# Spreading the second layer's decay rows with rounded-fp32 matmuls on 40 partitions

## The reference, cut to what matters

```
cum = jnp.cumsum(log_a.astype(jnp.float32).reshape(b, h, n, CHUNK), axis=-1)
decay = jnp.exp(jnp.where(lower, cum[..., :, None] - cum[..., None, :], -jnp.inf))
scores = jnp.einsum('bhnid,bhnjd->bhnij', qc, kc) * decay
y_intra = jnp.einsum('bhnij,bhnjv->bhniv', scores, vc)
```

## Time and profile before

| | us |
|---|---|
| median of 3 runs | 1595.27 |
| lowest and highest of them | 1591.41, 1597.74 |
| the profiled execution | 1586.63 |
| its span, first to last instruction | 1584.8 |
| PE busy in the span | 1465.9 |
| the second layer's mixer, from the first spread to the output projection | about 673 to 757 |
| mean granted TensorE clock, share of 2.4 GHz | 0.959 |

### The profile page before, as it was taken

How to read it: one execution, slowest core, us unless ns; L and a number is a source line. 1 busy time by engine, 2 the same in 40 slices (tenths; PEclk the granted TensorE clock), 3 DMA queues, 4 the chain that set the end, 5 groups by cost and what they waited for, 6 DMA issues and landing times.

```text
span 1584.8 us, 22300 instructions
## 1 busy us (share of the span) xinstructions
PE 1465.9 (92%) x8816; PEld 1227.8 (77%) x8816; DVE 933.9 (59%) x1539; ACT 669.0 (42%) x1079; POOL 783.5 (49%) x359
## 2 busy tenths in 40 slices
PE   5999878999989998885999999999999989899997
PEld 3878678999978887442778888888878854799997
DVE  3687657878786687557676544431127687634433
ACT  3446544454543233555342222222226366454443
POOL 0533315888844443644334444444444540478885
PEclk9999988999989999966999999999999999999999
DMA  9657405777765652000236555543333330345664
GB/s 369 232 196 268 159 11 183 245 254 246 250 221 177 196 161 89 19 27 1 80 114 217 187 186 186 186 140 98 97 98 100 105 100 1 107 148 186 186 182 124
DMA packets 71319, 242.96 MB, mean 153 GB/s; under 512 B 7472, under 2 KB 13104, under 8 KB 70832
## 3 DMA queue, kind: packets, MB, share of 16 engines
q1 hardware_dynamic: 68800, 237.15, 44.8%
q10 hardware_dynamic: 2416, 4.39, 0.9%
HBM read 239.42 MB, written 1.05 MB: 152 GB/s over the span
## 4 chain that ended last, share of the span: by engine, by line
PE 49%; DVE 5%; ACT 2%; issue 1%; POOL 1%; DMA 0%; DVEq 0%; ACTq 0%
PE bank L513 13%; PE bank L515 13%; PE bank L514 13%; PE bank L923 1%; POOL w_lo L1729 1%; PE cond_a L983 1%; DVE sq_sum L1843 1%; PE bank L646 1%; PE bank L647 1%; PE bank L650 1%; PE cond_b L1001 1%; PE cond_b L931 1%; DVE h_lo L1786 0%; PE bank L943 0%; PE cond_b L943 0%
## 5 line engine op out<-in xcount | busy, mean ns | idle before, releaser
L1729 POOL TENSOR_TENSOR w_lo<-raw,w_hi 128x1024 fp32r<-128x1024 f32 (+3 forms) x306 | 721.5, 2366 | 739.7 <-ACT w_hi L1231 724.7
L1231 ACT ACTIVATE w_hi<-raw 128x1024 fp32r<-128x1024 f32 (+3 forms) x301 | 309.4, 1030 | 598.6 <-PE bank L515 541.0
L513 PE MATMUL bank<-h_hi,w_hi 128*128 128x256 f32 (+2 forms) x1604 | 529.6, 330 | 8.8 <-POOL w_lo L1729 5.4
L514 PE MATMUL bank<-h_lo,w_hi 128*128 128x256 f32 (+2 forms) x1604 | 525.9, 328 | 0.0
L515 PE MATMUL bank<-h_hi,w_lo 128*128 128x256 f32 (+2 forms) x1604 | 525.8, 328 | 0.0
L513 PEld LDWEIGHTS bank<-h_hi,w_hi 128*128 128x128 f32 (+1 forms) x1604 | 301.9, 188 | 45.6 <-POOL w_lo L1729 6.4
L515 PEld LDWEIGHTS bank<-h_hi,w_lo 128*128 128x128 f32 (+1 forms) x1604 | 301.9, 188 | 30.2
L514 PEld LDWEIGHTS bank<-h_lo,w_hi 128*128 128x128 f32 (+1 forms) x1604 | 302.1, 188 | 29.9
L1786 DVE TENSOR_TENSOR hidden_lo<-work,hidden_hi 128x256 fp32r<-128x256 f32 (+1 forms) x66 | 113.2, 1715 | 162.2 <-ACT hidden_hi L1303 162.2
L513 PE MATMUL bank<-hidden_hi,w_hi 128*128 128x256 f32 (+1 forms) x528 | 168.7, 320 | 0.6 <-POOL w_lo L1729 0.6
L514 PE MATMUL bank<-hidden_lo,w_hi 128*128 128x256 f32 (+1 forms) x528 | 168.5, 319 | 0.0
(11 more groups left out here) (399 smaller groups left out, 1899.2 us busy)
## 6 DMA issues: line engine op xcount, KB each, us to landing
raw<-in_up SPq DMA_DIRECT2D x132, 512.0 KB, 3.6
ada_w<-in_ada SPq DMA_DIRECT2D x128, 512.0 KB, 4.5
raw<-in_down SPq DMA_DIRECT2D x48, 448.0 KB, 3.4
raw<-in_out SPq DMA_DIRECT2D x24, 512.0 KB, 3.6
raw<-in_down SPq DMA_DIRECT2D x24, 512.0 KB, 3.5
raw<-in_in SPq DMA_DIRECT2D x24, 512.0 KB, 3.6
arena<-in_ada SPq DMA_DIRECT2D x16, 512.0 KB, 11.8
raw<-in_uq SPq DMA_DIRECT2D x12, 384.0 KB, 3.0
```

Of the source, the lines that this page charges most:

```text
L513: pe.matmul(out, w_h, x_h, start=first, stop=False)
L514: pe.matmul(out, w_h, x_l, start=False, stop=False)
L1231: act.activation(part_slot(w_hi, f, u), raw_slot(f, u), ACT.Copy).then_inc(s["rounded"], 1)
L1729: pool.tensor_tensor(part_slot(w_lo, f, u), raw_slot(f, u), part_slot(w_hi, f, u).bitcast(F32), ALU.subtract).then_inc(s["split"], 1)
```

## The change

The rows of sums are split into a rounded high part and the low part that the rounding leaves, as is done for the weights, and both are spread by one fp32r matmul.

- PE makes the rows twice: for each 128 tokens one plain-fp32 matmul writes output partitions 0 to 31 (it takes 32 columns of the sums, of which the first 8 are the wanted ones), and one writes the same 8 rows to partitions 32 to 39. So 16 matmuls stand in place of 8.
- DVE copies 40 partitions instead of 8 into `grow`, which is now a view of fp32r type on the same memory (`work_r`), waits for its own second copy, and then subtracts the rounded rows from PSUM on partitions 32 to 39, in two instructions of 8x512.
- A new tensor `picks` (128x8, fp32r) is the sum of two slices of the identity: its column h is 1 on partitions h and 32 + h. The DVE instruction that makes it stands ahead of its wait for the running sums.
- `spread` takes column h of `picks[0:40]` and `grow[0:40]`: fp32r by fp32r, 40 partitions.

```diff
+        pick_rows = sbr("picks", [P, RH])
...
+        with nc.sbuf_tensor("work_r", [P, 3, TOK], F32R) as work_r:
+            pass
         work = sb("work", [P, 3, TOK])
...
-        gs, ngs = c(2, TT, RH), c(2, TT, RH)
+        sums_flat = c(4 * TT * RH)
+        gs, ngs = (sums_flat[:, 64 * a:64 * a + 64].rearrange("p (d i h) -> p d i h", d=2, i=TT) for a in range(2))
         v_mean, gn_inv, sq_2 = c(2, 4), c(32), c(512)
-        grow, dt_rows = work[:, 0:2, :], std
+        grow, dt_rows = work_r[:, 0:2, :], std
+        picks = pick_rows[:, :]
...
-                    pe.matmul(decay_bank(q)[:, :], ident[0:RH, h:h + 1].to_broadcast([RH, P]), grow[0:RH, d, :],
+                    pe.matmul(decay_bank(q)[:, :], picks[0:40, h:h + 1].to_broadcast([40, P]), grow[0:40, d, :],
                               start=True, stop=True).then_inc(s["sd_b"], 1)
...
-                        last = pe.matmul(bank[6 + d][0:RH, i * P:(i + 1) * P], gs[:, d, i, :], ident,
+                        n = (TT * d + i) * RH
+                        pe.matmul(bank[6 + d][0:32, i * P:(i + 1) * P], sums_flat[:, n:n + 32], ident,
+                                  start=True, stop=True)
+                        last = pe.matmul(bank[6 + d][32:40, i * P:(i + 1) * P], sums_flat[:, n:n + RH], ident,
                                          start=True, stop=True)
...
                 vr_products(5, 8)
+                then(dve.tensor_tensor(picks, ident[:, 0:RH], ident[:, 32:32 + RH], ALU.add))
                 dve.wait_ge(s["cum_ready"], 2)
...
-                copy(grow[0:RH, 0, :], bank[6][0:RH, :])
-                copy(grow[0:RH, 1, :], bank[7][0:RH, :]).then_inc(s["rows_taken"], 1)
+                copy(grow[0:40, 0, :], bank[6][0:40, :])
+                then(copy(grow[0:40, 1, :], bank[7][0:40, :]))
+                low(grow[32:40, 0, :], bank[6][32:40, :], grow[32:40, 0, :])
+                low(grow[32:40, 1, :], bank[7][32:40, :], grow[32:40, 1, :]).then_inc(s["rows_taken"], 1)
```

## The result

The changed kernel takes 1580.05 us (median of six runs, 1566.88 to 1584.44); the kernel before, on the same chip, takes 1594.49 (six runs, 1591.41 to 1599.77). The ratio is 0.9896, with a 95% interval from 0.9853 to 0.9939. By it the change is worth 16.6 us of 1594.49 (the two medians lie 14.4 apart), and the forecast was 6.5. Two later repetitions gave 0.992 and 0.9911, so 13 to 17 us is what has to be explained.

The account below looks back on a forecast made before the run. Hand-overs between engines, on a chain through PE's spreads, bound the mixer, with no engine full. Savings 3.30 + 0.24 + 2.03 + 1.06 = 6.6 us, costs 0, 6.5 with hand-overs: 1595.27 - 6.5 = 1588.8 us, range 1582 to 1595.

Parts of the forecast that it names:

- price of `picks`: One small DVE instruction of 0.17 us, placed where DVE idles 0.60 us waiting for PE: cost 0, at most 0.1 us.
- walk along the chain: Second layer's mixer, 672 to 757 us, in four pieces, asking what is late next: 6.6 us saved together.
- q = 4, 5: Mixer spreads, 692 to 707 us: DVE is late next, so of 1.3 us only 0.24 arrives.
- q = 8, 11: Mixer spreads, 707 to 722 us: an idle DVE waits for each, so 2.03 us arrives.
- q = 0 to 3: First mixer spreads, 672 to 692 us: PE runs without a gap, so all 3.30 us arrives.
- q = 12, 15: Mixer spreads, 722 to 757 us: 0.66 us, then about 0.4 as POOL is late next; sum 1.06.
- Price of one spread: A spread on the chain goes from 1.05 to 0.40 us at 2.4 GHz, from 2.07 to 0.71 at 1.2.
- Rows, subtractions, `picks`: Added PE and DVE work: DVE 1.45 us later, within its 1.70 us wait for POOL (the cover); cost 0, bounds to 3.4.
- higher bound of 1.75 us: Extra PE time for the rows if their 32 records run one after the other; the sum took 0.1 us instead.
- more of it at 1.2 GHz: Rival: more mixer spreads at 1.2 GHz, each saving 1.36 instead of 0.65 us; 8 to 11.5 us less, chance 0.25.
- the clock falls instead: Rival: shorter spreads leave the mixer's 2.4 GHz stretches at 1.2 GHz; net +5.5 us, 1601, chance 0.05.
- The signs: Expected after: 16 L1006 records, 0.2 us DVE wait, first spread at 673.3, stretch to L513 from 83.4 to about 77 us.

Follow-up runs that it names:

- e1: The kernel before plus one unused 32-byte tensor where the change puts `picks`, no instruction changed; ratio to the kernel before 0.996.
- e9: The changed kernel plus 64 more unused bytes behind `picks`, 96 in all; 1572.69 us against 1592.45 for the kernel before, ratio 0.9878.
- e4: The kernel before plus an unused tensor of 64 bytes in the place of `picks`; ratio to the kernel before 0.9965.
- e6: The change with `picks` behind all other tensors (old addresses), but spreads left plain fp32 on 8 partitions; ratio to the kernel before 1.0009.
- e2: The whole change with `picks` allocated behind `spare`, so all other tensors keep their old addresses; ratio to the kernel before 0.9941.
- e3: The changed kernel measured again, unaltered; ratio to the kernel before 0.992.
- e11: The changed kernel measured a third time, unaltered; 1580.78 us, ratio to the kernel before 0.9911.
- e10: The kernel before plus 32 unused bytes ahead of the weights, so weights and all else move together; ratio to the kernel before 1.0001.
- run 32: Not a run label: in "run 32 records in the 1.9 us", "run" is a verb and 32 counts matmul records.

## Why the prediction was wrong

Two terms failed. The price of `picks`, put at 0 and at most 0.1 us, took its one DVE instruction and left out its 32 bytes, which moved the operands of the dense matmuls: measured alone (e1), 6.4 us. And the walk along the chain, 6.6 us, kept all work between the spreads at its old duration, and let 0.24 and 2.03 us arrive at q = 4, 5 and q = 8, 11 where 0.9 and 2.5 did: the mixer got 9.4 us shorter.

**The walk.** In the table "long" is the mean of the eight traces with plain fp32 spreads, "short" of the five of the change. The pieces end at the prediction's borders: the first `group_spread` (692), `ssd_weighted` of pair 0 (707), `ssd_scores` of pair 1 (722), L513.

| piece | long | short | gained | forecast |
|---|---|---|---|---|
| q = 0 to 3 | 19.0 | 14.0 | 5.0 | 3.30 |
| q = 4, 5 | 15.8 | 14.9 | 0.9 | 0.24 |
| q = 8, 11 | 14.3 | 11.8 | 2.5 | 2.03 |
| q = 12, 15 | 34.8 | 33.7 | 1.0 | 1.06 |
| mixer | 83.8 | 74.4 | 9.4 | 6.6 |

- *Price of one spread:* right. 0.42 and 0.72 for the pair on the chain were 0.40 and 0.63 in the sum, 0.73 to 0.81 at 1.2 GHz were 0.71. The 40 rows of the spread cost what 128 do, so the columns set the time, as assumed.
- *q = 0 to 3:* mis-sized. The spreads gave 3.17 in the profiled pair, as forecast. L988 and the norm's products gave 1.70 + 0.59 = 2.3 more (in e9, where L988 stayed slow, some 1.6), by the clock. The sum kept every other duration as it was.
- *q = 4, 5 and q = 8, 11:* the order of sizes was right, each 0.5 to 0.7 too small. The wait of DVE that limits the fifth spread was read at one place of one trace; the eight traces differ by up to 3.8 us in this piece (e4 has 18.89), so a limit of 0.24 said more than a trace can. What of these two terms is clock can't be separated here.
- *q = 12, 15:* right, though the pieces of it vary by more than the difference.
- *Rows, subtractions, `picks`:* right, each. 1.9 us for 32 records, 1.29 for two subtractions, 0.28 left of the cover, and e6 measures the sum of their instructions at nothing. The Trainium skill ("TensorE: Matmul & The Clock Gate", Packing small matmuls) says that weight loads overlap with running matmuls only when they go to other rows of the array. The higher bound of 1.75 us, which the prediction read from it, did not come; these pairs don't agree with it, and neither do the dense stretches, where PEld is busy 281.62 of 340 us beside a PE that never stops, both on all 128 rows.
- *The clock:* I had it as a rival, "more of it at 1.2 GHz", with the right sign in its half sentence and the wrong mechanism in its price. It priced more spreads at the lower level (up to 11.5 us); what happened is that the other work of PE took some 2 us less. That the mixer's 9.4 us lie in that rival's band of 8 to 11.5 is luck. Its 11.5 also counts q = 4 as a full saving, where the walk lets 0.24 us arrive for q = 4 and 5 together; with seven full ones it would be 10.2. The rival "the clock falls instead" did not happen: the mixer's mean granted clock is 0.68 in the changed kernel, as before, and 0.70 to 0.72 in e2, e3, e9 and e11.
- *`picks`, its memory:* missing altogether. The mixer's 9.4 us alone would have put the time at 1585.9, in the range. The other 6.4 (e1) took it out, to about 1579.5. No step of the prediction asked whether the new array moves others; the allocation stands in the diff as one line ahead of `sq_sum`, and the streams it speeds up are most of the kernel.
- *The signs:* L1006 has its 16 records of 0.4 to 0.5 and 0.8 us, the rows and DVE's wait came as named, and the mixer is 74.9 instead of 77. The first spread started 14 us later than "673.3 as before", and that was not the rows: at 600 us, ahead of the whole stage, it was 11.0 us late already. e1 and e3, with the same addresses, were 8.8 and 11.0 late there, e2, with the old ones, 1.0. Absolute times of a trace were the wrong sign; the duration of the stage was the right one.

## What to carry to other kernels

When a change allocates an array, list what moves, and keep the old addresses in one version: otherwise one measures two changes. Here a pad of 96 bytes with no use was worth about as much as the whole rewrite of the spreads at the old addresses (0.9934 and 0.9941). And in a stage whose clock keeps changing level, what a shorter matmul saves is not only its own time; price the neighbours at both levels, let the band reach there, and compare traces whose clock did the same ahead of the stage.

## What was not expected of the hardware

- The rate of back-to-back fp32r matmuls changes with the distance in bytes from the stationary to the moving operand: remainders by 128 of 96, 0, 32 and 64 gave 0.2333, 0.2267, 0.2333 and 0.2289 us at 512 columns, and 0.1183, 0.1200, 0.1167 and 0.1178 at 256. The best remainder for one width is not the best for the other. Moving both operands leaves it as it was (e10), and so does a pad that moves neither (`cq_hi` in e1 and e4). Why it is so stays open.
- An fp32r spread on 40 rows costs what one on 128 rows does, 0.39 us behind another matmul, and pairs of plain fp32 matmuls with 32 and 8 columns, written to two groups of partitions, run 32 records in the 1.9 us that 16 took alone.
- The same mixer has 6 to 17 us less at 1.2 GHz when its 16 spreads are fp32r, and about as much at 2.4 GHz. The time at 1.2 varies by some 7 us between executions of one program (47.8, 41.0 and 44.4 for the changed kernel).
